# Placing the output matmuls of a two-layer convolution trunk between its projection steps, with the normalisations on VectorE alone

## The chip, the cores and the metric

The kernel runs on the eight cores of one Trainium2 chip. Every core takes one prompt sequence of 2048 tokens and 64 new decode tokens, 2112 tokens in all, and works alone: nothing is exchanged between cores. The time of an execution is that of the slowest core, in microseconds (us), and the figure quoted for a kernel is the median of its runs.

## The reference

```python
def hybrid_layer(x, ...):
    h = rmsnorm(x, norm_g)
    p = einsum('btd,de->bte', h, w_in)            # 1024 -> 7168
    a_val, a_gate, z_a, gb, gc, hb, z_b = split(p, 7 ways)
    u = a_val * sigmoid(a_gate)
    ca = causal_dwconv(u, buf_a, conv_a_w)        # width 31
    ca = head_layernorm(ca + conv_a_b, ...)       # over 128 channels of a head
    y_a = silu(ca) * silu(z_a)
    v = gc * hb
    cb = causal_dwconv(v, buf_b, conv_b_w)        # width 3
    y_b = gb * cb * silu(z_b)
    y = einsum('bte,ed->btd', concat([y_a, y_b]), w_out)   # 2048 -> 1024
    return x + y
# two such layers, then a final rmsnorm; the last rows of u and v are also returned
```

## The kernel before

Channels lie on the partitions, in eight groups of 128, and tokens in the free dimension, in five blocks (four of 424 tokens, the last of 416: 352 prompt and 64 decode tokens). `x_sb` keeps x in float32 and `h_sb` the normalised x in bfloat16, both for all tokens. `y_sb` holds only four groups of 128 gated channels, so the output projection of a layer is done in four rounds of four groups each.

A layer has a part A (eight heads) and a part B (eight channel groups). In part A each head j runs over the five blocks: `a_step` projects the gate, the value and z (8 matmuls each, lines 325 and 333), forms u on VectorE (line 540), and copies u into shifted replicas `rep` with four DMAs of the SP queue (line 557). The convolution of width 31 is done on TensorE (line 450), two blocks at a time, on every second step and two to three steps late; mean, variance, normalisation, silu and the product that writes `y_sb` (`st_mean`, `st_var`, `st_tt`, `st_silu`, `st_y`) follow one stage at a time in later steps. The decode tokens' convolution (`a_samp`, lines 427 to 436) runs on GpSimd (POOL) after a head's last block and writes through `acc_f`, the buffer in which part B also accumulates. In part B each group runs `b_step` over the five blocks: 32 matmuls for z, Bg, C and hb, a three-tap convolution on VectorE into `acc`, and the product into `y_sb`.

After heads 0 to 3, heads 4 to 7, groups 0 to 3 and groups 4 to 7 stands one output stage each, `out_round`: for each block 8 groups of 4 matmuls (one per output channel group m), each followed by an addition into `x_sb` on VectorE (line 401). Within the output stages of part A, `drain_hook` finishes the convolution pipeline at fixed places.

The normalisation has two halves. `rms_stats` squares x on ScalarE (ACT, line 344), sums over the channels with 8 matmuls (line 351), and forms the factor `rr_t` with Ln and Exp (lines 356 and 358). `rms_apply` multiplies: groups 3, 5 and 7 by a product on POOL (line 381) and a scaled copy on ACT (line 384), the others in one instruction on VectorE (line 387); the final one of the kernel also does group 1 in that way for all but the last block, and writes into staging buffers from which one DMA per group (line 391) stores y.

Weights come in tiles of 128x1024 into `NW` slots of `wsl`, with DMAs of the POOL queue (line 310), in the order of the list `wseq`; `w_get_batch(k)` takes the next k slots and starts loads up to `NW` tiles ahead of the batch's start. The order of instructions on every engine is the order in which the Python code calls `P.op`; waits are derived from reads and writes of the named resources. A load or product that waits on POOL holds back whatever stands behind it there, and the same on each engine.

## Time and profile before

| | |
|---|---|
| median of 3 runs | 1334.97 us (1334.41 to 1339.0) |
| the profiled execution | 1334.29 us, span of its slowest core 1332.7 us |
| spans of the eight cores | 1325.8 to 1332.7 us |
| TensorE (PE) busy | 1229.4 us (92%) |
| VectorE (DVE) busy | 753.2 us (57%) |
| ScalarE (ACT) busy | 553.2 us (42%) |
| GpSimd (POOL) busy | 309.9 us (23%) |
| mean granted TensorE clock of the cores | 0.976 to 0.982 |

The span is the time from the first to the last instruction of the slowest core. A busy share is that of all the span, and engines overlap. In the timelines below a line is a run of like instructions: its start, the time it took, engine, line of the kernel, operation, output and inputs, the number of instructions, and in brackets how long the engine had been idle before it and what ended that.

### The profile page before, as it was taken

The page shows a single profiled execution, that of the slowest core. Times are in us where ns is not written, and L with a number is a line of the kernel's source. Part 1 is how long each engine was busy: PE and PEld are TensorE (multiplying, and loading weights), DVE is VectorE, ACT ScalarE, POOL GpSimd, SP SyncE. Part 2 cuts the span into 40 slices and gives each one's busy share as a digit, 9 for nine tenths or more (in the row PEclk, how much of TensorE's full clock was granted, in tenths as well). Part 3 has the DMA queues.
Part 4 walks back from the last instruction along what each step waited for, and adds up shares of the span by engine and source line. Part 5 has one row for each costly group of instructions (what it writes and reads, how often), then busy time and mean ns, then how long its engine had stood idle before and what let it go on. Part 6 is the DMA issues. An engine that isn't in the chain of part 4 may idle for free.

```text
span 1332.7 us, 25104 instructions; the slowest of 8 cores (1325.8 to 1332.7 us)
## 1 busy us (share of the span) xinstructions
PE 1229.4 (92%) x8618; PEld 652.7 (49%) x8618; DVE 753.2 (57%) x1350; ACT 553.2 (42%) x811; POOL 309.9 (23%) x397
## 2 busy tenths in 40 slices
PE   3699999999999999999969999999999999999973
PEld 0245455545455555555524454554545555555530
DVE  2444465343766667666854437443475667666684
ACT  3766652667511110111466766176741111111164
POOL 2353331333401000001144333033341000001033
PEclk9799999999999999999989999999999999999996
DMA  9354443454232321112393543354413321122027
GB/s 249 88 107 93 101 100 72 102 114 101 58 44 42 54 33 33 32 33 43 30 184 74 115 98 65 82 114 97 104 37 44 64 33 32 33 33 44 13 106 164
DMA packets 89579, 102.10 MB, mean 77 GB/s; under 512 B 17328, under 2 KB 70704, under 8 KB 89392
## 3 DMA queue, kind: packets, MB, share of 16 engines
q0 software_dynamic: 20736, 37.76, 18.5%
q1 hardware_dynamic: 67904, 58.67, 17.4%
q10 hardware_dynamic: 816, 4.08, 1.6%
q8 instruction: 72, 1.18, 0.4%
q14 instruction: 51, 0.42, 0.1%
HBM read 92.41 MB, written 13.37 MB: 79 GB/s over the span
## 4 chain that ended last, share of the span: by engine, by line
PE 81%; DMA 5%; ACT 4%; issue 3%; POOL 3%; DVE 2%; SPq 1%; DVEq 0%; ACTq 0%; POOLq 0%
PE ps L325 70%; PE ps L450 8%; DMA rep<-ubuf 3%; PE ps L351 2%; POOL tt_t L381 2%; ACT sq L344 1%; DMA x_sb<-xT 1%; PE ps L463 1%; SPq L557 1%; DVE x_sb L401 1%; PE ps L333 1%; ACT L356 0%; DMA y_fm<-sz_t 0%; POOL acc L433 0%; POOL sz_t L381 0%
## 5 line engine op out<-in xcount | busy, mean ns | idle before, releaser
L325 PE MATMUL ps<-h_sb,wsl 128*128 128x424 bf16 (+1 forms) x4400 | 812.6, 342 | 3.8 <-ACT th_t L529 2.8
L325 PEld LDWEIGHTS ps<-h_sb,wsl 128*128 128x128 bf16 x4400 | 427.1, 98 | 365.5 <-issue 19.9
L325 PE MATMUL ps<-y_sb,wsl 128*128 128x424 bf16 (+1 forms) x1280 | 236.1, 343 | 10.1 <-DVE x_sb L401 5.3
L401 DVE TENSOR_TENSOR x_sb<-x_sb,ps 128x424 f32<-128x424 f32 (+1 forms) x320 | 180.6, 591 | 51.8 <-PE ps L325 33.2
L325 PEld LDWEIGHTS ps<-y_sb,wsl 128*128 128x128 bf16 x1280 | 124.7, 98 | 117.2 <-issue 17.4
L540 DVE SCALAR_TENSOR_TENSOR ubuf<-th_t,ps 128x424 bf16<-128x424 f32 (+1 forms) x80 | 46.6, 583 | 196.3 <-PE ps L325 96.0
L310 POOL DMA_DIRECT2D wsl<-w_in_r x112 | 60.7, 550 | 401.6 <-PE ps L325 386.6
L638 ACT ACTIVATE sz_t<-ps 128x424 f32<-128x424 f32 (+1 forms) x80 | 41.8, 522 | 263.2 <-PE ps L325 263.2
L450 PE MATMUL ps<-rep,wc 128*32 128x424 bf16 (+1 forms) x2560 | 120.4, 340 | 9.6 <-DMA rep<-ubuf 9.5
L427 POOL TENSOR_TENSOR acc<-usam,hista 128x992 f32<-128x992 bf16 x32 | 59.3, 1855 | 280.6 <-DVE oa_t L547 202.2
L669 DVE SCALAR_TENSOR_TENSOR acc<-ubuf,cw_b_sb,acc 128x424 f32<-128x424 bf16 (+1 forms) x192 | 112.1, 584 | 20.8 <-DVE acc L666 1.1
L651 DVE TENSOR_TENSOR ubuf<-ps,th_t 128x424 bf16<-128x424 f32 (+1 forms) x80 | 47.0, 587 | 133.8 <-PE ps L325 133.8
L647 ACT ACTIVATE th_t<-ps 128x424 f32<-128x424 f32 (+1 forms) x80 | 41.8, 522 | 191.7 <-PE ps L325 174.7
L433 POOL TENSOR_TENSOR acc<-acc 128x480 f32<-128x480 f32 (+3 forms) x128 | 92.5, 722 | 18.9 <-POOL acc L433 0.9
L450 PEld LDWEIGHTS ps<-rep,wc 128*32 128x32 bf16 x2560 | 65.5, 97 | 62.9 <-issue 27.8
L529 ACT ACTIVATE th_t<-ps 128x424 f32<-128x424 f32 (+1 forms) x80 | 41.8, 522 | 105.5 <-PE ps L325 95.3
L351 PE MATMUL ps<-sq,ones_s 128*128 128x424 bf16 (+1 forms) x120 | 39.1, 446 | 45.4 <-ACT sq L344 45.4
L493 DVE SCALAR_TENSOR_TENSOR tt_t<-ps,cbias,rstd_t 128x424 f32<-128x424 f32 (+1 forms) x80 | 48.8, 652 | 46.0 <-ACT rstd_t L486 45.8
L455 DVE CAST cb<-ps 128x424 bf16<-128x424 f32 (+1 forms) x80 | 45.5, 578 | 44.2 <-PE ps L450 44.1
L470 ACT ACTIVATE d<-ps,cbias 128x424 bf16<-128x424 f32 (+1 forms) x80 | 48.3, 609 | 51.5 <-PE ps L463 45.4
L387 DVE SCALAR_TENSOR_TENSOR h_sb<-x_sb,vecs_sb,rr_t 128x424 bf16<-128x424 f32 (+1 forms) x50 | 47.5, 1009 | 31.6 <-ACT rr_t L358 31.6
L381 POOL TENSOR_TENSOR tt_t<-x_sb,rr_t 128x424 f32<-128x424 f32 (+1 forms) x33 | 43.3, 1333 | 93.0 <-ACT rr_t L358 76.6
(62 smaller groups left out, 805.0 us busy)
## 6 DMA issues: line engine op xcount, KB each, us to landing
rep<-ubuf SPq DMA_DIRECT2D x256, 113.0 KB, 2.6
wsl<-w_in_r POOLq DMA_DIRECT2D x112, 256.0 KB, 5.8
wsl<-w_out_r POOLq DMA_DIRECT2D x32, 256.0 KB, 5.3
x_sb<-xT SPq DMA_DIRECT2D x16, 424.0 KB, 13.8
rep<-ubuf SPq DMA_DIRECT2D x64, 95.0 KB, 2.3
hista<-hist_a SPq DMA_DIRECT2D x16, 255.5 KB, 3.4
oa_copy<-sa_orig ACTq DMA_DIRECT2D x2, 1664.0 KB, 19.5
y_fm<-sz_t SPq DMA_DIRECT2D x15, 212.0 KB, 2.3
```

Source lines behind the costliest of these rows:

```text
L310: P.op("pool", (lambda e, i=i, s=s: e.dma_start(out=wsl[:, s, :], in_=wseq[i])), writes=[w_r[s]], chan=ch_w[s], name=f"wload{i}")
L325: ins = e.matmul(bank(bk, n), lhsT=l_, rhs=r_, start=(i == 0), stop=(i == len(pairs) - 1))
L351: ins = e.matmul(bank(bk, n), lhsT=ones_s[:], rhs=sq[:, s, i, 0:n], start=(kp == 0 and i == 0), stop=(kp == 3 and i == 1))
L381: P.op("pool", (lambda e, k=k, tmp=tmp: e.tensor_tensor(out=tmp, in0=x_sb[:, k, c0:c0 + n], in1=rr_t[:, rs, 0:n], op=ALU.mult)), reads=[x_ ...
L387: P.op("dve", (lambda e, k=k, dst=dst, gk=gk: e.scalar_tensor_tensor(out=dst, in0=x_sb[:, k, c0:c0 + n], scalar=gk, in1=rr_t[:, rs, 0:n], ...
L401: P.op("dve", (lambda e, bk=bk, m=m, c0=c0, n=n: e.tensor_tensor(out=x_sb[:, m, c0:c0 + n], in0=x_sb[:, m, c0:c0 + n], in1=bank(bk, n), op ...
L427: P.op("pool", (lambda e: e.tensor_tensor(out=prod[:, :, :], in0=win(e), in1=hista[:, UHN:UHN + WA].unsqueeze(2).broadcast_to([128, WA, 32 ...
L433: P.op("pool", (lambda e, n=n, h=h: e.tensor_tensor(out=prod[:, 0:n - h, :], in0=prod[:, 0:n - h, :], in1=prod[:, h:n, :], op=ALU.add)), r ...
L450: ins = e.matmul(psum[32 * q:32 * q + 32, bd, 0:npr], lhsT=w, rhs=rep[:, rp, q, 4 * m:4 * m + npr], start=(m == 0), stop=False, tile_posit ...
L470: P.op("act", (lambda e: e.activation(out=d2[:, i2, 0:n], in_=bank(bd, n), func=AF.Square, bias=cbc)), reads=[bank_r[bd], cbias_r], writes ...
L493: P.op("dve", (lambda e: e.scalar_tensor_tensor(out=tt_t[:, it, 0:n], in0=bank(bd, n), scalar=cbc, in1=rstd_t[:, t, 0:n], op0=ALU.add, op1 ...
L669: P.op("dve", (lambda e, a0=a0, a1=a1, vsl=vsl, wcol=wcol, k=k: e.scalar_tensor_tensor(out=acc[:, iac, a0:a1], in0=vsl(k), scalar=wcol, in ...
```

## The change

- `out_round` and `drain_hook` go. `out_block` does one block of the output matmuls, and is called after a projection step: for heads 0 to 3 after each `a_step` of head 4; for heads 4 to 7 after each `b_step` of group 0; for groups 0 to 3 and 4 to 7 one block behind the `b_step`s of groups 3 and 7, with the last block after them. The list of weights is reordered to match, and `NW` is 10, not 9.
- The stages of the convolution pipeline are gathered in `pipe`, which runs on through all eight heads and the first four steps of group 0 in part B. Steps that share TensorE's output banks with it use banks 0 to 3 only, and so do the output matmuls placed there.
- All normalisations are on VectorE. The final one is written over `x_sb`, and stored with one DMA per two groups.
- The normalisation of layer 1 (and the final one) is done for blocks 0 to 3 within group 7's steps of the part before.

```diff
-NW = 9
+NW = 10
...
+        for j in range(8):
+            wseq.extend(w_in_r[l, c] for c in (8 + j, j, 16 + j))
+            if j == 4:
+                w_out_of(l, 0)
+        for j in range(8):
+            wseq.extend(w_in_r[l, c] for c in (48 + j, 24 + j, 32 + j, 40 + j))
+            if j in (0, 3, 7):
+                w_out_of(l, {0: 4, 3: 8, 7: 12}[j])
...
-                P.op("pool", (lambda e, k=k, tmp=tmp: e.tensor_tensor(
-                    out=tmp, in0=x_sb[:, k, c0:c0 + n], in1=rr_t[:, rs, 0:n], op=ALU.mult)),
-                    reads=[x_r[k][b], rr_r[rs]], writes=[tres])
-                P.op("act", (lambda e, tmp=tmp, dst=dst, gk=gk: e.activation(out=dst, in_=tmp, func=AF.Copy, scale=gk)),
-                     reads=[tres, vecs_r], writes=[dres])
...
+    def final_apply(b, rs, ks=range(KC)):
+        c0, n = BLOCKS[b]
+        for k in ks:
+            P.op("dve", (lambda e, k=k: e.scalar_tensor_tensor(
+                out=x_sb[:, k, c0:c0 + n], in0=x_sb[:, k, c0:c0 + n], scalar=vecs[:, 64 + k:65 + k],
+                in1=rr_t[:, rs, 0:n], op0=ALU.mult, op1=ALU.mult)),
+                reads=[x_r[k][b], rr_r[rs], vecs_r], writes=[x_r[k][b]])
+            if k % 2:
+                P.op("sp", (lambda e, k=k: e.dma_start(out=y_fm[:, k - 1:k + 1, c0:c0 + n], in_=x_sb[:, k - 1:k + 1, c0:c0 + n])),
+                     reads=[x_r[k - 1][b], x_r[k][b]], chan=ch_out[k // 2])
+
+    def out_block(b, slots, next_bank, hook=None):
+        c0, n = BLOCKS[b]
+        for m in range(KC):
+            bk = next_bank()
+            pairs = [(wsl[:, slots[kk], m * 128:(m + 1) * 128], y_sb[:, kk, c0:c0 + n]) for kk in range(4)]
+            mm_group(bk, n, pairs, reads=[w_r[s] for s in slots] + [y_r[kk][b] for kk in range(4)])
+            P.op("dve", (lambda e, bk=bk, m=m: e.tensor_tensor(
+                out=x_sb[:, m, c0:c0 + n], in0=x_sb[:, m, c0:c0 + n], in1=bank(bk, n), op=ALU.add)),
+                reads=[bank_r[bk], x_r[m][b]], writes=[x_r[m][b]])
+            if hook is not None:
+                hook(m)
...
+            slots, _ = w_batch(7 if j == 4 else 3)
...
+                    w_prefetch((6, 9, NW)[b - 2])
+                if j == 4:
+                    ob = Rot([1, 2, 3, 0] if st["g"] % 2 == 0 else [0, 1, 2, 3])
+                    out_block(b, slots[3:7], ob.next)
...
+            outs = j in (0, 3, 7)
+            slots, release = w_batch(8 if outs else 4)
...
+            def out_norm(b):
+                def hook(m):
+                    if j == 7 and b >= 1:
+                        if b == NB - 1 and m == 2:
+                            rs_of[b - 1] = rms_stats(b - 1, pool_all.next())
+                        if m >= 4:
+                            norm(b - 1, rs_of[b - 1], [2 * m - 8, 2 * m - 7])
+                out_block(b, slots[4:8], pool_all.next, hook)
+
+            for b in range(NB):
+                if j == 0:
+                    g = 8 * NB + b
+                    write_y = b_step(l, j, b, slots[0:4], g)
+                    if b == NB - 1:
+                        release(4)
+                    ob = Rot([2, 3, 0, 1] if g % 2 == 0 else [0, 1, 2, 3])
+                    out_block(b, slots[4:8], ob.next)
+                    write_y()
+                else:
+                    b_step(l, j, b, slots[0:4])()
+                    if outs and b == NB - 1:
+                        release(4)
+                    if j == 7 and b >= 2:
+                        rs_of[b - 2] = rms_stats(b - 2, pool_all.next())
+                    if outs and b >= 1:
+                        out_norm(b - 1)
+            if outs and j:
+                out_norm(NB - 1)
```

Where the instructions now stand, at three places (each row is an instruction, or xN like ones; the brackets name semaphores it waits for, `c_w5` being the load into weight slot 5 and `s_pe` TensorE). Line numbers of the changed kernel are its own: its lines 413 to 422 are `a_samp`, 373 the final normalisation, 387 the addition into x.

POOL, from the start of the kernel, before:

```order
L310 DMA wsl<-w_in_r 128x1024 x3
L381 TENSOR_TENSOR tt_t<-x_sb,rr_t 128x424 x12
L310 DMA wsl<-w_in_r 128x1024 x3
L381 TENSOR_TENSOR tt_t<-x_sb,rr_t 128x416 x3
L310 DMA wsl<-w_in_r 128x1024 x3
L427 TENSOR_TENSOR acc<-usam,hista 128x992
```

and in the changed kernel:

```order
L310 DMA wsl<-w_in_r 128x1024 x9
L413 TENSOR_TENSOR acc<-usam,hista 128x992
L419 TENSOR_TENSOR acc<-acc 128x480
L419 TENSOR_TENSOR acc<-acc 128x256
L419 TENSOR_TENSOR acc<-acc 128x128
```

The products of the normalisation that stood between the first loads are gone, so nine loads stand in a row at the start where three did.

POOL at the end of part A of layer 0 (the last decode convolution and the loads behind it), before:

```order
L436 TENSOR_TENSOR cbs<-acc 128x32 [waits s_pool]
L310 DMA wsl<-w_in_r 128x1024 [waits c_w7,s_pe]
L310 DMA wsl<-w_in_r 128x1024 [waits s_pe,c_w8]
L310 DMA wsl<-w_in_r 128x1024 [waits c_w0,s_pe]
L507 TENSOR_TENSOR y_sb<-tt_t,sz_t 128x424 [waits s_act]
```

and in the changed kernel, followed by TensorE at the first step of part B there:

```order
L419 TENSOR_TENSOR acc<-acc 128x64 [waits s_pool]
L422 TENSOR_TENSOR cbs<-acc 128x32 [waits s_pool]
L310 DMA wsl<-w_out_r 128x1024 [waits c_w5,s_pe]
L310 DMA wsl<-w_in_r 128x1024 [waits s_pe,c_w6]
L310 DMA wsl<-w_in_r 128x1024 [waits c_w7,s_pe]
```

```order
L325 MATMUL ps<-h_sb,wsl 128x424 [waits s_act,c_w8]
L325 MATMUL ps<-h_sb,wsl 128x424 x7
L325 MATMUL ps<-d,ones_v 128x424 [waits s_act,s_dve]
L325 MATMUL ps<-d,ones_v 128x424 [waits s_act]
L325 MATMUL ps<-h_sb,wsl 128x424 [waits c_w9]
L325 MATMUL ps<-h_sb,wsl 128x424 x7
L325 MATMUL ps<-h_sb,wsl 128x424 [waits c_w0,s_act]
L325 MATMUL ps<-h_sb,wsl 128x424 x7
L325 MATMUL ps<-h_sb,wsl 128x424 [waits c_w1,s_dve]
L325 MATMUL ps<-h_sb,wsl 128x424 x7
L325 MATMUL ps<-y_sb,wsl 128x424 [waits c_w2,c_w4,c_w3,c_w5,s_act]
```

The load into slot 5, an output weight, stands behind the whole decode convolution on POOL, and the first output matmul of part B waits for it after one step of 34 matmuls; before, the three loads there were for tiles used after a whole output stage.

VectorE at the end of the kernel (the last output block of layer 1 and what follows), before:

```order
L401 TENSOR_TENSOR x_sb<-x_sb,ps 128x416 x8
L387 SCALAR_TENSOR_TENSOR sz_t<-x_sb,vecs_sb,rr_t 128x424 x3
L387 SCALAR_TENSOR_TENSOR tt_t<-x_sb,vecs_sb,rr_t 128x424
L387 SCALAR_TENSOR_TENSOR rstd_t<-x_sb,vecs_sb,rr_t 128x416
L387 SCALAR_TENSOR_TENSOR th_t<-x_sb,vecs_sb,rr_t 128x416
L387 SCALAR_TENSOR_TENSOR sz_t<-x_sb,vecs_sb,rr_t 128x416 x3
```

and in the changed kernel:

```order
L387 TENSOR_TENSOR x_sb<-x_sb,ps 128x416 x5
L373 SCALAR_TENSOR_TENSOR x_sb<-x_sb,vecs_sb,rr_t 128x424 x2
L387 TENSOR_TENSOR x_sb<-x_sb,ps 128x416
L373 SCALAR_TENSOR_TENSOR x_sb<-x_sb,vecs_sb,rr_t 128x424 x2
L387 TENSOR_TENSOR x_sb<-x_sb,ps 128x416
L373 SCALAR_TENSOR_TENSOR x_sb<-x_sb,vecs_sb,rr_t 128x424 x2
L387 TENSOR_TENSOR x_sb<-x_sb,ps 128x416
L373 SCALAR_TENSOR_TENSOR x_sb<-x_sb,vecs_sb,rr_t 128x424 x2
L373 SCALAR_TENSOR_TENSOR x_sb<-x_sb,vecs_sb,rr_t 128x416 x8
```

The last block's additions are now mixed with the eight normalisations of the block before, and eight more follow for the last block where VectorE did five.

## Rows read from the trace of the kernel before

**Rows 1.** Waits of TensorE, whole span: total us, times, longest
```profile
PE ps L351 <- ACT sq L344: 45.4, 23, 7.0
PE ps L450 <- DMA rep<-ubuf: 9.5, 5, 3.1
...
PE ps L325 <- DVE x_sb L401: 6.3, 6, 1.2
PE ps L325 <- POOL y_sb L507: 4.8, 4, 1.3
```

**Rows 2.** Busy time in a 20 us stretch of part B
```profile
540.00:560.00 20.00, 20.00 (x115) 10.96 (x112) 12.70 (x27) 3.80 (x8) 2.11 (x4) 1.00 0.33 54
```

**Rows 3.** DMA issues of the first 30 us: KB each, us to landing
```profile
x_sb<-xT SPq DMA_DIRECT2D x16, 424.0 KB, 13.8
...
wsl<-w_in_r POOLq DMA_DIRECT2D x3, 256.0 KB, 13.3
```

**Rows 4.** Timeline of the first head of layer 0
```profile
43.62 3.03 PE L325 MATMUL ps<-h_sb,wsl 128*128 128x424 bf16 x16
...
44.82 5.47 DVE L387 SCALAR_TENSOR_TENSOR h_sb<-x_sb,vecs_sb,rr_t 128x424 bf16<-128x424 f32 x5 [7.05 <-ACT rr_t L358]
...
49.91 0.50 ACT L569 ACTIVATE sz_t<-ps 128x424 f32<-128x424 f32 x1
...
59.15 1.59 PE L325 MATMUL ps<-h_sb,wsl 128*128 128x424 bf16 x8 [0.88 <-ACT th_t L529]
...
62.35 0.51 ACT L569 ACTIVATE sz_t<-ps 128x424 f32<-128x424 f32 x1
...
66.92 4.42 PE L450 MATMUL ps<-rep,wc 128*32 128x424 bf16 x64
...
71.98 2.89 DVE L387 SCALAR_TENSOR_TENSOR h_sb<-x_sb,vecs_sb,rr_t 128x416 bf16<-128x416 f32 x5
...
79.82 4.66 PE L325 MATMUL ps<-h_sb,wsl 128*128 128x416 bf16 x16
```

**Rows 5.** Timeline of TensorE, first output stage of layer 0 and around it
```profile
84.41 3.05 PE L450 MATMUL ps<-rep,wc 128*32 128x424 bf16 x64
...
183.43 4.46 PE L325 MATMUL ps<-y_sb,wsl 128*128 128x424 bf16 x24
...
218.23 13.06 PE L325 MATMUL ps<-h_sb,wsl 128*128 128x424 bf16 x72
```

**Rows 6.** Timeline of POOL at the same place
```profile
182.69 1.85 POOL L427 TENSOR_TENSOR acc<-usam,hista 128x992 f32<-128x992 bf16 x1 [18.44 <-DVE oa_t L547]
...
194.60 1.66 POOL L310 DMA_DIRECT2D wsl<-w_in_r x3 [0.31 <-issue]
```

**Rows 7.** DMA issued between 193.5 and 195 us, to landing
```profile
wsl<-w_in_r POOLq DMA_DIRECT2D x1, 256.0 KB, 3.9
```

**Rows 8.** Timeline of TensorE from layer 0 into layer 1
```profile
665.80 1.60 PE L333 MATMUL ps<-h_sb,wsl 128*128 128x424 bf16 x8
...
674.43 2.98 PE L333 MATMUL ps<-h_sb,wsl 128*128 128x424 bf16 x8 [3.29 <-DVE ubuf L540]
...
712.79 3.05 PE L450 MATMUL ps<-rep,wc 128*32 128x424 bf16 x64
```

**Rows 9.** Timeline of the last 75 us
```profile
1260.29 9.48 PE L325 MATMUL ps<-y_sb,wsl 128*128 128x424 bf16 x52
...
1264.79 6.66 DVE L401 TENSOR_TENSOR x_sb<-x_sb,ps 128x424 f32<-128x424 f32 x13
...
1291.17 3.29 ACT L344 ACTIVATE sq<-x_sb 128x848 bf16<-128x848 f32 x4
...
1316.94 0.69 SPq L677 DMA_DIRECT2D ob_new<-ob_t  x1
...
1318.07 0.55 ACT L358 ACTIVATE rr_t<-rr_t 128x416 f32<-128x416 f32 x1
```

**Rows 10.** DMA issues from 1309 us on
```profile
ob_new<-ob_t SPq DMA_DIRECT2D x1, 256.0 KB, 11.0
```

More of the change, by code:

```diff
@@ L268, in build_nc @@
     ch_rep = [chan(f"rep{i}") for i in range(NR)]
-    ch_out = [chan(f"out{i}") for i in range(NTH + NSZ + 4)]
+    ch_out = [chan(f"out{i}") for i in range(4)]
     ch_oa = chan("oa")
@@ L515, in a_step @@
         sg, sv, szw = st["slots"]
-        odd = g % 2
         last = b == NB - 1
         npr = NPL if last else n
-        bg, bv, bz = (1, 2, 3) if odd else (0, 1, 0)
-        pair = []
-        if odd and len(q_conv) >= 2:
-            pair = [q_conv.pop(0), q_conv.pop(0)]
-            for s in pair:
-                st_conv(s)
-            while q_y:
-                st_y(q_y.pop(0))
+        bg, bv, bz = (1, 2, 3) if g % 2 else (0, 1, 0)
+        pipe(0, g)
         proj(sg, b, bg, by_k)
@@ L559, in a_step @@
         rep_r[rp].w = P.ops["sp"][-1]
[L560 to L566 removed]
+        pipe(2, g)
         proj(szw, b, bz)
@@ L632, in b_step @@
         s_zb, s_gb, s_gc, s_hb = slots
-        bzb = pool_all.next()
+        if g is None:
+            bzb, bgb, bgc, bhb = [pool_all.next() for _ in range(4)]
+        else:
+            bzb, bgb, bgc, bhb = (2, 3, 2, 3) if g % 2 else (0, 1, 0, 1)
+            pipe(0, g)
         proj(s_zb, b, bzb)
@@ L639, in b_step @@
              reads=[bank_r[bzb]], writes=[sz_r[isz]])
-        bgb = pool_all.next()
+        if g is not None:
+            pipe(1, g)
         proj(s_gb, b, bgb)
@@ L643, in b_step @@
              reads=[bank_r[bgb], sz_r[isz]], writes=[sz_r[isz]])
-        bgc = pool_all.next()
+        if g is not None:
+            pipe(2, g)
         proj(s_gc, b, bgc)
@@ L686, in build_nc, with w_batch @@
     rs_of = {}
+    def w_batch(k):
+        start = wstate["next"]
+        return w_get_batch(k), (lambda dead: w_prefetch(start + dead + NW))
     for l in range(DEPTH):
```

217 lines of the change are left out of this document (69 added, 148 removed).

## The prediction

> **What bounds the kernel now.** I read the busy shares first, then the waits of TensorE, then its timeline at each place where the program changes its shape. TensorE is busy for 92% of the span, and inside a stage of part B nothing holds it: 114 to 115 matmuls in 20 us at the full clock, 0.175 us each, while VectorE is busy for 12.7 of the 20 us and ACT for 3.8 [rows 2]. The work of TensorE is the same in both kernels, so the change can only win or lose at the seams. The reader is to see four kinds of seam. Statistics of x that wait for the squares of ACT cost 45.4 us in 23 waits; the output stages of part A cost 6.3 us of waits for VectorE's additions and 4.8 for POOL's products; five convolutions wait for their replicas, 9.5 us [rows 1]. The rest is idle time and low clock at the start, from layer 0 to layer 1, and at the end [rows 4, 8, 9].
>
> **The change, part by part.** All against the profiled execution's 1334.3 us, which is 0.7 us below the median of the runs shown.
>
> *Start.* With the scaled copies off ACT, the silu of z no longer waits for them. In one step the projection of z ended at 46.65 and its silu began at 49.91, 3.3 us later; in the next it ended at 60.74 and the silu began at 62.35, 1.6 later [rows 4]. The squares of the next statistics stand behind that silu on ACT, and TensorE behind the squares, so both come off the path, and about 1 us in the step before them. From the first convolution at 66.92 to the next at 84.41 are 17.5 us [rows 4, 5], for 52 matmuls at 0.175 and one pair of convolutions of 3.0, 12.1 us in all; of the 5.4 lost, part is waiting for ACT's copies and part matmuls at half rate (16 in 4.66 us at 79.82, against 3.03 at 43.62 [rows 4]). I take 4. VectorE's eight multiplications cost no more than its five did: five took 5.47 us with POOL at work beside them, and 2.89 us, 0.58 each, without [rows 4], so eight are 4.6. Block 1's squares can start up to 4 us earlier, if x is there; against that, POOL now issues nine weight loads at once instead of three, and the first three, sharing the DMA engines with x, took 13.3 us to land while the x transfers took 13.8 [rows 3]. I take 2 for this. Start: minus 12. Ends: minus 16 if the loads disturb nothing, 0 if x is late by all of them (six loads at about 1.9 us, from three that land within 6 us of one another's issue at 194.60).
>
> *Output stages of part A.* One stage spans 183.43 to 218.23, 34.8 us [rows 5], for 165 matmuls and a pair of convolutions, about 32. The waits behind the difference are the 6.3 and 4.8 us of [rows 1]. After head 4's steps the same matmuls find four banks that are read at once and products that were written a step earlier, with VectorE needed for some 7 of 12 us of a step. Minus 11; ends minus 11 and minus 5.
>
> *Replicas.* Four of the five waits fall on the third step after a weight load that starts when POOL has finished the decode convolution; heads 2 and 6 keep that phase. One goes, minus 2 (0 to minus 4).
>
> *Layer 0 to layer 1.* From 665.80 to 712.79 are 47.0 us [rows 8] for 140 matmuls and 3.0 of convolutions, 27.5: 19.5 us lost to four normalisations between the projection steps. In the changed kernel one is left there. It costs 2.8: silu 0.5, first square 0.8, then three squares at 0.82 (four take 3.29 [rows 9]) against two matmuls at 0.35. Three more now stand right behind a `b_step`, where ACT starts squaring while TensorE still does the 1.4 us of hb: 1.5 us of idle time each, 4.5. The fourth meets a VectorE that is behind: four additions at 0.51 (13 take 6.66 [rows 9]) and eight multiplications at 0.58 against 2.8 us of matmuls leave the last addition of block 3 about 3.4 us late, 2.7 us idle; and the first u of layer 1 queues behind the rest, 1.2. Loss 11.2, gain 8 (3 to 12). VectorE is not the bound before that: 3.5 + 4.1 + 4.6 = 12.2 us a step, TensorE 12.6 + 1.5.
>
> *End.* All projections end at 1260.3 [rows 9]. From there, with four output blocks and three statistics, 152 matmuls at 0.177 and 4.5 idle: block 3 is out at E = 1291.7. Then VectorE sets the time. Its last addition for block 3 comes at E + 3.4, the factor for block 3 at E + 6.1, and the mixed row of additions and multiplications runs on to the last addition of block 4 at E + 12.1; squares, sums, Ln and Exp give the last factor at E + 14.9 = 1306.6, against 1318.6 [rows 9]. Eight multiplications end at E + 19.5. The last transfers: before, 14.1 us passed from factor to end, and the `ob_new` store issued at 1316.94 took 11.0 us to land [rows 9, 10]; now it is issued at E + 14.5 and would land at E + 25.5, with the last pairs of groups about then. End at 1317.2, minus 15.5. Ends: 14.1 us after the factor as before, minus 12; last store landed 2.6 us after its product, minus 19.
>
> *What it adds: the first output matmul of part B waits for its weight.* The group needs four tiles; the fourth is loaded by POOL only after the decode convolution of head 7. At the same place of the loop before, the last projection of the head ended at 183.4 [rows 5], POOL had begun the convolution at 182.69 and issued its next load at 194.60, 11.2 us after that end [rows 6], and the first tile landed 3.9 us later [rows 7]: 15.1 to 15.5. TensorE has 34 matmuls until then, 6.0 us. So 9.4 us of idle time in each layer, behind which everything in part B stands, since nothing else is queued on TensorE. Before, those loads had a whole output stage to hide them, 34.8 us [rows 5]; that cover is gone. `acc`, which the decode convolution holds as well, is free earlier and costs nothing more. After an idle time of 3.3 us the next 8 matmuls took 2.98 us, at the lower of the clock's two levels, in place of 1.4 [rows 8]: 2 us more here. Then each of the five steps has four banks for its output matmuls and VectorE does the v product and three taps first, 2.4 + 0.6 us before the first bank is free against 2.8 of matmuls: 0.3 a step, 1.5 a layer. Plus 13 a layer, 26; ends plus 20 and plus 32.
>
> Sum: −12 − 11 − 2 − 8 − 15.5 + 26 = −22.5, so **1312**.
>
> **A rule that speaks against it.** What the rows show is that three loads and the transfers of x were in flight together for 13 us [rows 3]; my 2 us for the start supposes that x loses little to six more. The Trainium skill (DMA: Bandwidth & Descriptors, section on queues, rings and completion order) says that each DMA engine goes round robin, packet by packet, between the queues that have work. By that rule the six loads are taken in while x is still arriving, x comes later by up to their whole time, and the sum would be 1324 in place of 1312. No run here shows nine loads at once.
>
> **The rivals.**
> - *x late by all six loads.* For: DMA engines are saturated there and POOL has nothing between the loads. Against: the ACT chain, not the arrival of x, sets the steps after block 1. The start gains nothing: 1324. Chance 0.13.
> - *No stall at part B.* If the tile came in time, the 20 us and their clock would not be paid: about 1289. For it only that a load can be faster than the one seen; against it 11.2 us of POOL's work in front of it. 0.06.
> - *VectorE becomes the bound in group 7's steps.* If a multiplication costs 1.09 us (5.47 for five [rows 4]) also there, a step needs 16.3 us of VectorE against 14.1 of TensorE, in three steps of two layers, and the end loses 8: 13 + 8 = 21, 1333. Against: POOL, which ran beside those five, only issues loads there. 0.11, of which a third stops short at about 1326.
> - *Slower: TensorE falls to 1.2 GHz in the mixed steps of part B.* The idle time comes at their head, and short bank waits follow in each step. The ten steps are some 120 us at the full clock; with half of that time's work at the lower level they cost 60 more: 1372. It turns the result from 29 us on, which is a quarter of the work there. For: matmuls at half rate after 3.3 us idle [rows 8]. Against: the next 16 there ran at full rate. 0.08.
>
> **How the numbers follow.** The forecast itself has 0.62, and its own bounds taken together give 1301 to 1323. The range for 8 in 10 reaches a little past them to the case of late x: 1299 to 1326. A measurement of this kernel can tell about 0.5% from no change, 6.7 us, so faster means below 1328.3: 0.62 + 0.13 + 0.06 + 0.04 = 0.85. Same: 0.07. Slower: 0.08.
>
> **What would show it.** In the profile of the changed kernel: two waits of TensorE, 8 to 11 us each, at the first output matmul of part B, ended by a weight load; no wait for POOL's products; the first convolution near 56 us and not 66.9; one normalisation's wait of some 3 us after layer 0; the last factor near 1307 less what the rest moved (so 14 us or less before the end). The prediction is wrong if those two waits are under 5 us, if the first convolution stays at 66, if the clock stays low in the mixed steps, or if VectorE's multiplications cost over 0.8 us.

## The result, and the profile after

The changed kernel takes **1367.9 us** (median of 4 runs) against 1335.2 for the one before on the same chip: ratio 1.0235, interval 1.0210 to 1.0261. It is slower by 33 us where 22.5 less was forecast, and lies outside the range. In some executions of any of these kernels the cores of one die or both show a lower granted clock and the time is longer (here the fourth, 1387.0); ratios and intervals leave these out, the medians do not. The profiled execution took 1368.1 us, with a span of 1366.5 on its slowest core.

TensorE's waits in the changed kernel (us in total, times, longest), beside [rows 1]:

```profile
PE ps L351 <- ACT sq L344: 40.3, 46, 3.8
PE ps L436 <- DMA rep<-ubuf: 31.0, 7, 8.7
PE ps L325 <- DMA wsl<-w_out_r: 18.8, 2, 9.5
...
PE ps L325 <- DVE x_sb L387: 8.2, 10, 1.6
PE ps L325 <- ACT sz_t L564: 3.2, 6, 0.7
```

The two waits for an output weight are the predicted ones (9.4 each), and the one for POOL's products is gone. What the sum did not have is the second line: the convolutions' replicas cost 31.0 us where they cost 9.5. Four places on TensorE's timeline of the changed kernel show the largest of these waits and one of the two for the tile, with what follows them:

```profile
260.35 3.02 PE L436 MATMUL ps<-rep,wc 128*32 128x424 bf16 x32 [8.13 <-DMA rep<-ubuf]
...
361.33 8.27 PE L325 MATMUL ps<-y_sb,wsl 128*128 128x424 bf16 x32 [9.30 <-DMA wsl<-w_out_r]
...
720.47 5.05 PE L436 MATMUL ps<-rep,wc 128*32 128x424 bf16 x64 [8.66 <-DMA rep<-ubuf]
...
910.18 3.02 PE L436 MATMUL ps<-rep,wc 128*32 128x424 bf16 x32 [5.40 <-DMA rep<-ubuf]
```

The number in brackets is the idle time before the row. The 32 matmuls after 9.30 us of it took 8.27, and 32 at the full rate take 5.8 (52 in 9.48, [rows 9]): the idle time costs 2.4 us more behind itself. The convolutions pay likewise: 64 matmuls took 5.05 us where 64 take 3.05 [rows 5]. In front of the first row, at head 5 of layer 0, the DMA traffic of the changed kernel from 243 to 262 us reads so (KB each, us to landing):

```profile
q0 software_dynamic: 1008, 1.84, 62.9%
q1 hardware_dynamic: 1126, 0.91, 16.9%
...
wsl<-w_in_r POOLq DMA_DIRECT2D x7, 256.0 KB, 10.1
rep<-ubuf SPq DMA_DIRECT2D x8, 113.0 KB, 9.9
```

POOL issues seven loads in a row there, at 243.89: head 4 now uses seven tiles (three projections and four of output), and head 5 refills their slots at once. The replica copies in flight with them need 9.9 us. The wait before 910.18 is that of head 5 in layer 1. In front of 720.47 it is another transfer (688 to 722 us of the changed kernel):

```profile
q10 hardware_dynamic: 96, 3.41, 54.3%
q0 software_dynamic: 576, 1.05, 17.9%
q1 hardware_dynamic: 1808, 1.56, 14.6%
...
oa_copy<-sa_orig ACTq DMA_DIRECT2D x2, 1664.0 KB, 19.1
rep<-ubuf SPq DMA_DIRECT2D x12, 113.0 KB, 16.1
wsl<-w_in_r POOLq DMA_DIRECT2D x4, 256.0 KB, 23.3
```

The queues' rows are packets, MB and share of the DMA engines: `oa_copy` (q10) moves 3.41 MB in 96 packets, 35 KB each, beside weight loads (q0) of 1.8 KB a packet and replicas (q1) of 0.9, which take 16 us to land. It was issued at the same point of the program before, within the last block of output matmuls, but then the first convolution of layer 1 was further away. The copy and that convolution in the kernel before, and the copy in the changed kernel:

```profile
664.58 1.32 ACTq L742 DMA_DIRECT2D oa_copy<-sa_orig  x2
...
697.55 3.14 PE L450 MATMUL ps<-rep,wc 128*32 128x424 bf16 x64
```

```profile
690.21 1.33 ACTq L728 DMA_DIRECT2D oa_copy<-sa_orig  x2
```

Before, 33.0 us lay between them; in the changed kernel TensorE has nothing else to do from 711.8 on, 21.6 us after the issue, because three of the four normalisations no longer stand between these steps. It was the normalisations that covered the copy, not an output stage.

The start: the first two convolutions of the changed kernel stand at 67.93 and 80.87, where [rows 4, 5] have 66.92 and 84.41, so 3.5 us are won of the 12.

```profile
67.93 3.66 PE L436 MATMUL ps<-rep,wc 128*32 128x424 bf16 x64
...
80.87 3.05 PE L436 MATMUL ps<-rep,wc 128*32 128x424 bf16 x64
```

That is what the prediction named as a sign of being wrong: the first convolution is not near 56. In its first 45 us x shares the DMA engines with nine weight loads. From 15 to 30 us the engines (last two columns: their busy share and GB/s) read so in the changed kernel, and, below it, in the experiment start_loads, where only three loads are issued before x has landed:

```profile
15.00:30.00 15.00, 2.59 (x6) 0.41 (x6) 5.75 (x9) 4.72 (x6) 0.00 (x0) 1.00 1.05 220
```

```profile
15.00:30.00 15.00, 9.29 (x28) 2.92 (x28) 7.69 (x14) 8.73 (x12) 0.00 (x0) 1.00 1.00 306
```

The engines are busy throughout in both, but with the nine loads they move 220 GB/s in all and not 306: x loses the bytes of the six extra loads and part of the rate besides.

The end: the last block's factor and what follows it, in the changed kernel, beside [rows 9, 10]:

```profile
1351.02 0.79 SPq L639 DMA_DIRECT2D ob_new<-ob_t  x1
1351.56 0.55 ACT L358 ACTIVATE rr_t<-rr_t 128x416 f32<-128x416 f32 x1
1352.21 4.59 DVE L373 SCALAR_TENSOR_TENSOR x_sb<-x_sb,vecs_sb,rr_t 128x416 f32<-128x416 f32 x8 [2.20 <-ACT rr_t L358]
1353.49 4.16 SPq L378 DMA_DIRECT2D y_fm<-x_sb  x4
```

The multiplications cost 0.57 us each as forecast. From the factor (1352.1) to the end are 14.4 us, as before (14.1), not the 11 of the sum.

Where the 33 us are, by landmarks that both kernels have: the second convolutions of the two layers (80.87 above and 734.80, for 84.41 and 712.79 in [rows 5, 8]) and the first projection of group 4 of part B, before and then after:

```profile
518.00 114.40 PE L325 MATMUL ps<-h_sb,wsl 128*128 128x424 bf16 x640
...
1146.05 114.40 PE L325 MATMUL ps<-h_sb,wsl 128*128 128x424 bf16 x640
```

```profile
537.75 97.31 PE L325 MATMUL ps<-h_sb,wsl 128*128 128x424 bf16 x544
...
734.80 3.05 PE L436 MATMUL ps<-rep,wc 128*32 128x424 bf16 x64
...
1190.08 97.31 PE L325 MATMUL ps<-h_sb,wsl 128*128 128x424 bf16 x544
```

Both stretches to group 4 get half of the sum's terms for the output stages, the replicas and part B.

| stretch | before | changed | difference | forecast |
|---|---|---|---|---|
| start to second convolution, layer 0 | 84.4 | 80.9 | -3.5 | -12 |
| to group 4 of part B, layer 0 | 433.6 | 456.9 | +23.3 | +6.5 |
| to second convolution, layer 1 | 194.8 | 197.1 | +2.3 | -8 |
| to group 4 of part B, layer 1 | 433.3 | 455.3 | +22.0 | +6.5 |
| to the end | 186.7 | 176.4 | -10.2 | -15.5 |

### The profile page after: what moved, and what is told of

Same layout as the page of the kernel before. It is cut to its first block, busy times and chain, and to the rows that moved or that the text cites. A ratio compares the mean times of both kernels' runs of the same rounds, so it can differ in the third digit from the quotient of the medians.

```text
span 1366.5 us, 24760 instructions; the slowest of 8 cores (1355.9 to 1366.5 us)
## 1 busy us (share of the span) xinstructions
PE 1234.1 (90%) x8618; PEld 652.9 (48%) x8618; DVE 747.3 (55%) x1407; ACT 531.2 (39%) x768; POOL 236.5 (17%) x340
## 4 chain that ended last, share of the span: by engine, by line
PE 76%; DMA 8%; DVE 5%; ACT 4%; issue 3%; POOL 1%; SPq 1%; DVEq 0%; ACTq 0%; POOLq 0%
PE ps L325 66%; PE ps L436 8%; DMA rep<-ubuf 5%; DMA x_sb<-xT 2%; ACT sq L344 2%; DVE x_sb L387 2%; SPq L558 1%; PE ps L333 1%; DVE x_sb L373 1%; PE ps L449 1%; POOL acc L419 1%; DVE h_sb L365 1%; PE ps L351 1%; DMA wsl<-w_out_r 1%; POOL acc L413 1%
## 5 line engine op out<-in xcount | busy, mean ns | idle before, releaser
L325 PE MATMUL ps<-y_sb,wsl 128*128 128x424 bf16 (+1 forms) x1280 | 241.4, 346 | 29.7 <-DMA wsl<-w_out_r 18.8
L387 DVE TENSOR_TENSOR x_sb<-x_sb,ps 128x424 f32<-128x424 f32 (+1 forms) x320 | 176.2, 589 | 32.5 <-PE ps L325 21.6
L597 ACT ACTIVATE sz_t<-ps 128x424 f32<-128x424 f32 (+1 forms) x80 | 41.8, 522 | 323.3 <-PE ps L325 311.4
L436 PE MATMUL ps<-rep,wc 128*32 128x424 bf16 (+1 forms) x2560 | 126.1, 350 | 31.0 <-DMA rep<-ubuf 31.0
L351 PE MATMUL ps<-sq,ones_s 128*128 128x424 bf16 (+1 forms) x120 | 35.6, 392 | 40.6 <-ACT sq L344 40.3
L602 DVE TENSOR_TENSOR sz_t<-ps,sz_t 128x424 f32<-128x424 f32 (+1 forms) x80 | 47.4, 593 | 31.4 <-PE ps L325 29.7
```

Source lines behind the costliest of these rows:

```text
L325: ins = e.matmul(bank(bk, n), lhsT=l_, rhs=r_, start=(i == 0), stop=(i == len(pairs) - 1))
L351: ins = e.matmul(bank(bk, n), lhsT=ones_s[:], rhs=sq[:, s, i, 0:n], start=(kp == 0 and i == 0), stop=(kp == 3 and i == 1))
L387: P.op("dve", (lambda e, bk=bk, m=m: e.tensor_tensor(out=x_sb[:, m, c0:c0 + n], in0=x_sb[:, m, c0:c0 + n], in1=bank(bk, n), op=ALU.add)), ...
L436: ins = e.matmul(psum[32 * q:32 * q + 32, bd, 0:npr], lhsT=w, rhs=rep[:, rp, q, 4 * m:4 * m + npr], start=(m == 0), stop=False, tile_posit ...
L602: P.op("dve", (lambda e: e.tensor_tensor(out=sz_t[:, isz, 0:n], in0=bank(bgb, n), in1=sz_t[:, isz, 0:n], op=ALU.mult)), reads=[bank_r[bgb] ...
```

## The experiments

Theory: the placement is harmless, and what costs is that four sets of transfers and one tile come at the wrong moment. Rival: the placement between steps itself, by its banks, its statistics and TensorE's clock. Each run was timed beside the kernel before on the same chip. The medians of before were 1334.8 us for the first four runs and 1335.0, 1333.2 and 1339.7 for the later ones, so runs of different sets are compared by ratio; a ratio less by 0.001 is 1.3 us.

| run | us | ratio to before | interval |
|---|---|---|---|
| changed kernel | 1367.9 | 1.0235 | 1.0210 to 1.0261 |
| tile_early | 1360.4 | 1.0194 | 1.0180 to 1.0208 |
| loads_paced | 1350.4 | 1.0114 | 1.0099 to 1.0129 |
| copy_late | 1359.2 | 1.0188 | 1.0175 to 1.0202 |
| start_loads | 1362.7 | 1.0202 | 1.0185 to 1.0219 |
| tile_early_acc | 1350.2 | 1.0116 | 1.0101 to 1.0132 |
| ob_early | 1364.6 | 1.0232 | 1.0217 to 1.0247 |
| all_five | 1307.9 | 0.9796 | 0.9783 to 0.9810 |
| before_dve_norm | 1308.1 | 0.9818 | 0.9798 to 0.9839 |
| all_six | 1306.1 | 0.9796 | 0.9776 to 0.9815 |
| norm_paced | 1288.2 | 0.9651 | 0.9629 to 0.9673 |
| norm_plain | 1318.8 | 0.9891 | 0.9873 to 0.9910 |
| six_banks | 1296.6 | 0.9700 | 0.9668 to 0.9731 |
| stats_mid | 1300.6 | 0.9727 | 0.9700 to 0.9754 |
| all_nine | 1292.1 | 0.9656 | 0.9623 to 0.9690 |
| norm_over_x | 1295.2 | 0.9683 | 0.9652 to 0.9714 |

### One cause at a time

**tile_early.**
```diff
         if last:
+            if j == 7:
+                w_prefetch(wstate["next"] - 3 + NW + 1)
             a_samp(0)
```


> Changed kernel, with the eighth tile of part B's first group loaded before the decode convolution of head 7 in POOL's program instead of after it. Late tile theory: the two waits for the w_out tile (9.3 and 9.5 us) go. In their place stays what the decode convolution still holds, the accumulators of VectorE's taps, behind which the additions of the output blocks are queued: POOL is done 11.2 us after the last projection, TensorE has 32 matmuls (5.6 us) and four banks (2.8 us) until then, so a wait of 3 to 5 us for VectorE. Gain 5 a layer and 1 to 2 of clock: 1356 (1353 to 1360) against 1367.9. Rival, that the accumulators alone would hold TensorE as long: 1366 to 1368, with waits of 8 us or more for VectorE at the same place.

Measured 1360.4, by ratio 5.5 us under the changed kernel. The waits for the tile are gone; `acc` takes their place, as one row of VectorE's waits (345 to 385 us) and one of TensorE's timeline in this run show:

```profile
DVE acc L630 <- POOL cbs L422: 3.0, 1, 3.0
```

```profile
359.67 4.71 PE L325 MATMUL ps<-y_sb,wsl 128*128 128x424 bf16 x16 [3.51 <-DVE x_sb L387]
```

**tile_early_acc.**
```diff
-        iac = rot_acc.next()
+        if g is None:
+            iac, av, ar = rot_acc.next(), acc, acc_r
+        else:
+            iac, av, ar = rot_rr.next(), rr_t, rr_r
```
(and `av`, `ar` for `acc`, `acc_r` in the taps and the product)

> The kernel of run tile_early (1360.4 us), and in part B's first group the products with the taps are kept in the two buffers of the normalisation factor, which nothing uses there, instead of in the buffers that the decode convolution of head 7 holds. If those buffers are what VectorE still waits for (its wait for POOL was 3.0 us at the first tap, TensorE's for VectorE's additions behind it 3.5 and 4.9 us): these waits go, and the matmuls at half rate behind them: minus 9 (7 to 12), 1351. Rival, that the four banks and VectorE's own work at this place make the same wait, whoever holds the buffers: minus 0 to 3, 1358 to 1360.

Measured 1350.2, another 10 us. The prediction's sentence that `acc` "costs nothing more" held only while the tile was late as well: tile and buffers are the same 9.4 us, held by the same decode convolution.

**loads_paced.**
```diff
+                if paced and 1 <= b <= 3:
+                    w_prefetch(goal - (todo * (3 - b)) // 3, [rep_r[st["rep"]]])
```
(`goal` is what the head's start would have loaded, `todo` how many that is; the list is what the load waits for)

> Changed kernel, with the weight loads of part A's heads 1 to 7 not issued all at the head's start but spread over its second to fourth block, each waiting until the replicas of that block have landed. Collision theory (the loads that head 5 issues seven in a row take the DMA engines from the replica copies): the waits for replicas at heads 5 and 6 (8.1, 2.5, 1.7 us in layer 0; 5.4, 2.8 in layer 1) fall under 1 us each, and the matmuls at half rate behind them go: minus 20 (16 to 25), 1348. The wait of 8.7 at the start of layer 1 and the two for the w_out tile stay (or grow by up to 1 us). Rival, that the copies wait for their queue on SP or for the u of VectorE, whatever POOL loads: no change of those waits, 1366 to 1369.

Measured 1350.4, with the layer 1 wait left alone, as expected, in TensorE's waits of this run:

```profile
PE ps L325 <- DMA wsl<-w_out_r: 20.0, 2, 11.3
PE ps L436 <- DMA rep<-ubuf: 12.0, 3, 7.8
```

So some 16 us (17.5 by the medians) were paid to loads that nothing needed at once. The edit spreads the loads of all these heads and not only head 5's; of the changed kernel's waits, the 8.1 and 5.4 us behind the seven loads are the largest that went. The rival falls: same copies, same SP queue, other loads.

**copy_late.**
```diff
-        if l == 0:
-            for l2 in range(DEPTH):
-                P.op("act", ... oa_copy[l2] ...)
+                if l == 1 and b == 4 and j in (1, 2):
+                    P.op("act", ... oa_copy[j - 1] ...)
```


> Changed kernel, with the two oa_copy transfers (3.4 MB, from memory to memory) issued in part B of layer 1 instead of just before the first step of layer 1. If oa_copy is what the first replicas of layer 1 collide with: the wait of 8.7 us at 720.47 falls to 0 to 2 and its matmuls at half rate go: minus 9 (7 to 11), 1359. If the four weight loads issued at 693.60 do as much by themselves: the wait stays at 4 us or more, 1363 to 1367. Should oa_copy disturb the place where it now stands, a wait for a weight tile shows there; none is expected, since part B has no replicas.

Measured 1359.2, by ratio 6.3 us less. On the slowest core the first convolutions of layer 1 then start without a wait:

```profile
712.44 4.15 PE L436 MATMUL ps<-rep,wc 128*32 128x424 bf16 x64
```

The four weight loads beside it, still there, do no harm that can be seen. The rule by which the prediction argued (the Trainium skill, DMA: Bandwidth & Descriptors, section on queues, rings and completion order: each engine takes the queues in turn, packet by packet) fits this. With turns by packet, 35 KB against 0.9 leaves little for the replicas. No run here changes the packet size alone.

**start_loads.**
```diff
-                    w_prefetch((6, 9, NW)[b - 2])
+                    w_prefetch((6, 9, NW)[b - 2], [x_r[7][NB - 1]])
```


> Changed kernel, with the seven weight loads that POOL issues during the first head of layer 0 made to wait until the last piece of x has landed. If the loads are what makes x late: the last x piece lands 6 to 10 us earlier, block 1's squares start earlier, and the first two convolutions (67.93 and 80.87) move forward by 6 to 9: 1360 (1357 to 1363). Rival, that x is limited by its own 20 issues on SP, which take 39.7 us: no change in either landmark, 1367 to 1369.

The first convolutions moved by 10.2 us, to where the prediction had wanted the first (56):

```profile
57.71 3.67 PE L436 MATMUL ps<-rep,wc 128*32 128x424 bf16 x64
...
70.66 3.05 PE L436 MATMUL ps<-rep,wc 128*32 128x424 bf16 x64
```

The time fell by 5.2 only, and by ratio by 4.4, with intervals that just overlap; the waits for replicas are still there and a core's come out differently (8.7 to 13.4 us in layer 0 in this run, on two cores). The pair norm_plain and before_dve_norm below shows the same edit at 9.7 us by ratio.

**ob_early.** `b_finish(l)` stands right behind the last `b_step`.

> Changed kernel, with the two stores of ob issued as soon as the last step of part B has made their data, before the stores of y for block 3, and not between those of block 3 and block 4. If the end is set by what all stores of the last 15 us move together: the 0.26 MB of ob_new in 1024 pieces leave the last stretch, the four stores of block 4 land in 6 to 8 us instead of 8.9, minus 2 (1 to 4): 1366. Rival, that the four stores of block 4 take 8.9 us by themselves: no change, 1367 to 1369.

Median 1364.6, but the intervals of the ratio overlap: no gain in time is shown by this run. Its profile does show the mechanism. The last four stores, from issue to landing, in the changed kernel and in this one:

```profile
y_fm<-x_sb SPq DMA_DIRECT2D x4, 416.0 KB, 8.9
```

```profile
y_fm<-x_sb SPq DMA_DIRECT2D x4, 416.0 KB, 2.5
```

The end comes 7.8 us after the factor, not 14.4, so the rival falls. In all_five it comes 8.1 us after it.

### All of it, and the other half of the change by itself

> Changed kernel with all of it together: paced loads (now also in head 0 of layer 1), oa_copy in part B of layer 1, the seven first loads after x, the eighth tile before head 7's decode convolution with separate buffers for part B's first taps, and the ob stores early. If the losses are separate places that add up: 1367.9 minus 7.5, 17.5, 8.7 and 5.2 as measured one by one, minus 9 for the buffers and 2 for the ob stores: 1318 (1312 to 1324), faster than the kernel before. The waits for replicas are then under 1 us each, those for the w_out tile gone, and what is left of TensorE's waits is the statistics' 30 to 40 us. Rival, that the placement of output matmuls between steps costs something of its own (banks, clock), which the waits hid: 1330 to 1345, with the clock under 0.98.

Measured 1307.9. The edits are those above together, with the pacing in every head of part A but the first (`l + j > 0`). This is below the expected range: taken as measured (with 10.2 for the buffers and 3.3 for the ob stores) the losses promised 1316, and by ratio only 1323. Together they gain 8 to 15 us more than one by one, and which of them does isn't shown; the pacing of head 0 of layer 1, new here, is one candidate. The next run shows that as much can be won without the placement.

**before_dve_norm.**
```diff
-            rms_apply(0, 0, rs_of[0], split=(3, 5, 7))
+            rms_apply(0, 0, rs_of[0])
```
(and so in the four other calls; the first loads wait for `x_r[7][NB - 1]`)

> Kernel before, its output stages as they were, with the normalisations all on VectorE (final ones too, through their staging buffers as before) and the six loads that would then be issued at once made to wait for the last piece of x. This is the part of the change that the prediction gave 12 us at the start. If that mechanism is right and only the loads spoiled it in the changed kernel: the first convolution moves from 66.92 to 56 to 58 and the time falls by 8 to 12: 1325 (1322 to 1328). If the start is bound by x and nothing is won: 1334. At the end eight multiplications on VectorE in place of a split between two engines may cost up to 2.

Measured 1308.1: minus 27 (24 by ratio), and not 8 to 12, with the old output stages, the old loads but for the first six, and the old `oa_copy`. The places, in its timeline (TensorE and, last, the end of its statistics):

```profile
69.80 3.05 PE L450 MATMUL ps<-rep,wc 128*32 128x424 bf16 x64
...
167.84 4.46 PE L325 MATMUL ps<-y_sb,wsl 128*128 128x424 bf16 x24
...
696.30 3.05 PE L450 MATMUL ps<-rep,wc 128*32 128x424 bf16 x64
...
1243.15 7.15 PE L325 MATMUL ps<-y_sb,wsl 128*128 128x424 bf16 x39
...
1283.83 0.85 PE L351 MATMUL ps<-sq,ones_s 128*128 128x416 bf16 x2 [0.48 <-ACT sq L344]
```

Against 84.41 and 183.43 [rows 5] the start gives 15; from there to 712.79 [rows 8] two more; and from the first output matmul of the last stage (1260.29 [rows 9]) to the last sum this kernel takes 41.5 us, where the one before took 57 (its factor follows at 1318.07). Of this 10.8 reach the end of the kernel. The rest is lost behind the last sum, where 20.1 us pass to the end instead of 15.3, with the `ob` stores still in front of the last ones (in norm_paced below, with these issued early, 10.4). Without scaled copies ACT squares while TensorE works, and TensorE's waits for squares go from 45.4 to this:

```profile
PE ps L351 <- ACT sq L344: 23.6, 29, 2.8
PE ps L450 <- DMA rep<-ubuf: 13.4, 5, 5.2
```

**norm_plain** is the same without the guard on the loads.

> The kernel of run before_dve_norm (1308.1 us) without the wait for x in front of the six first loads, so that nine are issued at once as in the changed kernel. If they make x late also here: the first convolution goes from 56.7 to 62 to 67, and the time rises by 4 to 7: 1313 (1311 to 1316), still faster than the kernel before. Rival, no difference: 1307 to 1309.

Measured 1318.8: the loads cost 9.7 us here by ratio (10.7 by the medians). This is the normalisation half of the change as it was written, and it is 1.1% faster than the kernel before; the other half is then what loses 46 us (ratio 1.0235 less 0.9891). The guard on the loads was not tried on the kernel before by itself, so what it would give with the old normalisations stays open.

**all_six** moves one more load.
```diff
-        if l == 0:
-            P.op("act", ... histb ...)
+                if l == 0 and j == 6 and b == 3:
+                    P.op("act", ... histb ...)
```
Its reason is a row of all_five, of VectorE's waits from 320 to 345 us:

```profile
DVE ubuf L581 <- DMA histb<-hist_b: 9.3, 1, 9.3
```

> The kernel of run all_five (1307.9 us), and the load of part B's history issued in head 6 of part A instead of at the start of part B. In all_five VectorE waits 9.3 us for that load at part B's first step, TensorE 6.0 us behind it (333.77), and 8 matmuls at half rate follow. If nothing else holds that place: these go, minus 7 to 8, 1300 (1297 to 1303). Rival, that the next thing (the accumulators, the banks) makes a wait of its own of 4 us or more there: 1304 to 1308.

Measured 1306.1, ratio unchanged. The wait for the history is gone, others stand in its place on the slowest core (TensorE's timeline in layer 0 and 1):

```profile
335.26 4.55 PE L325 MATMUL ps<-y_sb,wsl 128*128 128x424 bf16 x16 [2.18 <-DVE x_sb L387]
...
899.21 0.31 PE L449 MATMUL ps<-cb,ones_n 128*128 128x352 bf16 x1 [4.53 <-POOL cbs L422]
```

The second is made by my own pacing: the load of the fourth block waits for its replicas, and the decode convolution is queued behind it on POOL.

**norm_paced** is before_dve_norm, so with the old output stages, and with the diffs of loads_paced, copy_late and ob_early.

> The kernel of run before_dve_norm (1308.1 us; output stages of their own), and with it the paced loads of part A, oa_copy in part B of layer 1 and the ob stores early, that is the same cures as in all_five and all_six but without the placement of output matmuls between steps. Its waits for replicas (13.4 us, 5.2 of it at 681.73) and the half rate behind them go, and some of the last stores' time: 1297 (1294 to 1301). The difference to all_six is what the placement between steps is worth by itself: by the prediction's terms for the output stages of part A and for part B's banks some minus 8, which would leave this kernel behind all_six by as much; if it is worth nothing, the two agree within 3 us.

Measured 1288.2, 3.5% under the kernel before, and 18 under all_six, on the same chip: with its transfers mended, the placement still costs 18 us, where the expectation had it ahead by 8. By the landmarks of both profiles (slowest cores): second convolution 68.62 against 71.73; from there to the same convolution in layer 1 618.0 against 624.3; from there to the last sum 589.7 against 599.7. The first of these is not the placement's: both kernels start alike but for one weight load, and on the cores of these two profiles that convolution comes anywhere from 68.6 to 71.8.

### What the placement costs

**six_banks** and **stats_mid**, each on all_six:
```diff
-                    ob = Rot([2, 3, 0, 1] if g % 2 == 0 else [0, 1, 2, 3])
+                    ob = Rot([[2, 3, 4, 5, 0, 1, 4, 5], [0, 1, 4, 5, 2, 3, 4, 5], [2, 3, 4, 5, 6, 7, 0, 1],
+                              [0, 1, 4, 5, 6, 7, 2, 3], [2, 3, 0, 1, 4, 5, 6, 7]][b])
```
```diff
-                        if b == NB - 1 and m == 2:
+                        if m == 2:
                             rs_of[b - 1] = rms_stats(b - 1, pool_all.next())
...
-                    if j == 7 and b >= 2:
-                        rs_of[b - 2] = rms_stats(b - 2, pool_all.next())
```


> The kernel of run all_six (1306.1 us), with the output matmuls in part B's first group going round six to eight banks instead of four. If the banks are the cost: the ten waits for VectorE's additions there (0.6 to 2.2 us, some 13 in all) fall to 4 or less, minus 9: 1297 (1295 to 1300). Rival, that VectorE is behind by its own work and the wait only moves to the next projection: minus 0 to 3, 1303 to 1306.

> The kernel of run all_six, with the sums of the squares in head 7 of part B placed behind the third output matmul group of the next block instead of right behind the projection step. If TensorE waits there because ACT starts to square only then (four waits of 0.24 to 0.28 us a statistics and matmuls of 2 in 0.8 us instead of 0.35): each statistics gains 1.8, three in each layer, minus 9: 1297 (1295 to 1300). Rival, that the factor comes later and VectorE's multiplications with it, so that the end is pushed out: 1304 to 1308.

By ratio 0.0096 (12.8 us) and 0.0069 (9.2 us) under all_six. TensorE's waits for VectorE's additions in six_banks, 13.0 in all_six:

```profile
PE ps L325 <- DVE x_sb L387: 4.0, 4, 1.8
```

And one statistics of the last stretch, first in all_six, then in stats_mid:

```profile
1259.58 0.52 PE L351 MATMUL ps<-sq,ones_s 128*128 128x424 bf16 x2 [0.28 <-ACT sq L344]
1260.38 0.52 PE L351 MATMUL ps<-sq,ones_s 128*128 128x424 bf16 x2 [0.28 <-ACT sq L344]
```

```profile
1256.87 1.60 PE L351 MATMUL ps<-sq,ones_s 128*128 128x424 bf16 x8
```

In the first TensorE gets two matmuls every 0.8 us, at ACT's pace; in the second all eight run in 1.6.

**all_nine** has both, and `if paced and b <= 2` in place of `1 <= b <= 3`.

> The kernel of run all_six with both (six_banks and stats_mid) and the paced loads one block earlier, so that the decode convolution no longer stands behind a load that waits for the fourth block's replicas. If these three are the 18 us by which the placement is behind: minus 9, 9 and 3 (the 4.5 us wait for POOL at 899.21 goes): 1286 (1282 to 1290), level with norm_paced. If something else costs it: 1295 or more.

Ratio 0.9656, beside 0.9651 for norm_paced: level, within the 4 us or so that these intervals can tell. The three together are the 18 us, though less than their sum (12.8, 9.2 and the expected 3), and the earlier loads were not tried alone. They don't win anything beyond the old stages either.

**norm_over_x** is norm_paced with `final_apply` of the changed kernel, and the same pacing as all_nine.

> The kernel of run norm_paced (1288.2 us; output stages of their own, normalisations on VectorE), with the final normalisation written over x and stored in pairs of channel groups, as in the changed kernel, and the paced loads one block earlier. The end takes as long by the profile of both (10.4 us from the last sum to the end), so the first does nothing: minus 0 to 2; the paced loads: minus 1 to 2 for the waits behind POOL and VectorE: 1286 (1283 to 1289).

Ratio 0.9683, with an interval that overlaps norm_paced's. Written over x or through staging buffers: no gain is shown, and a loss of a few us isn't excluded.

## Why the prediction was wrong

- *Stall at part B's first output matmul, plus 26:* right in place, cause and size (9.3 and 9.5 us for 9.4; the half rate behind it 2.4 for 2). Its side remark on `acc` was wrong (above). Its banks were priced 1.5 a layer and cost 4.1 (8.2 us in ten waits); in all_six the waits for additions are 13.0 us, nearly all there, and six_banks gains 9 to 13.
- *Replicas, minus 2:* **this step failed, and it alone turns the sign.** I looked at the phase of the waits and took the loads as they had been: three or four at a time. The change makes head 4 use seven tiles, so head 5 issues seven loads, and it takes three of the four normalisations away that lay between `oa_copy` and layer 1's first convolution. The waits went from 9.5 to 31.0 us, plus 21.5 where minus 2 stood, and the half rate behind four of them adds some 6 (3.02 us for 1.62 three times, 5.05 for 3.05). The two cures, each by itself, gain 22 us by ratio and 26 by the medians. With plus 28 in this place the sum is plus 7; what is missing to the measured 33 is the start, the output stages with the banks, and the end.
- *Start, minus 12:* the mechanism was right, and larger than priced (15 in before_dve_norm); the six early loads took it back. Of the two prices weighed, 2 us and all of it, the second was near: 10 us at the first convolution. That rival was named, with 0.13, and by it the sum would have been 1324. Its rule from the Trainium skill (DMA: Bandwidth & Descriptors, section on queues, rings and completion order: the queues are taken in turn, packet by packet) agrees with the trace in that x comes later while the loads are taken in; that the whole rate falls too, 220 GB/s for 306, the rule does not say.
- *Output stages of part A, minus 11:* less than half of it, and lost again. If the tile, the banks and the replicas are taken off the two stretches of plus 23.3 and plus 22.0, an estimated minus 5 is left; the banks cost 8.2 where 3 were priced, and all_six, with its tiles in time, takes 6.3 us more over layer 0 than norm_paced. What the stages lose (up to 1.3 us a wait [rows 1]) the placement loses in banks and silus.
- *Layer 0 to 1, minus 8:* the size was right, and it belongs to the normalisations. From the end of part B's first group to the second convolution of layer 1 the changed kernel takes 311.4 us against 309.5, with 8.7 of wait for `oa_copy` and 2 of half rate in it: minus 9 without them. Before_dve_norm has the same gain without the placement, and loses it to the same wait (5.2 us, then 64 matmuls in 5.30 us instead of 3.05): 27.0 us lie there between the issue of the copy and the end of TensorE's other work, where the kernel before had 33.0 and the changed one 21.6.
- *End, minus 15.5:* measured minus 10.2. The factor comes 10.5 us earlier against group 4, for 12 in the sum; the statistics behind each step go at ACT's pace. The end after the factor is as long as before and not 3.5 shorter, because the two `ob` stores go out right before the last four stores and all of them land together 9 to 11 us later. Before_dve_norm gained 10.8 there with the old stage, so the placement itself gives nothing at the end.
- *The rivals:* VectorE as bound did not come, nor did TensorE at 1.2 GHz through the ten mixed steps: in the changed kernel the last column but two, the granted clock, is 0.93 over the stretch with the stall, and full behind it. The forecast of 0.08 for slower named the wrong mechanism; 1367.9 being near its 1372 is chance.

```profile
350.00:425.00 75.00, 61.20 (x374) 32.04 (x375) 44.67 (x86) 13.99 (x21) 9.78 (x17) 0.93 0.19 28
425.00:560.00 135.00, 135.00 (x758) 73.95 (x757) 86.03 (x167) 19.82 (x38) 9.44 (x18) 1.00 0.24 40
```

## What to carry to other kernels

When a change moves work between stages, list every transfer by the gap between its issue and the next wait that shares the DMA engines with it: the output stage that was taken away was the cover of the history load and of a weight tile, the normalisations that went were that of `oa_copy`, and the larger batch of tiles became a burst of seven loads. Loads that are early enough anyway should be issued one by one, behind the small copies that are urgent. And take a change apart before judging it: here one half wins 1.1% as written and 3.5% with its transfers in order, while the other half hides it under 46 us, and no gain of its own is shown when it is mended.

## What the runs showed of the hardware that I had not expected

- Two transfers of 1.7 MB from memory to memory, in 35 KB packets, held up replica copies of 113 KB for 16 us (2.6 us without them, in copy_late), while the four weight loads of 256 KB in 1.8 KB packets cost no wait when they stood there alone. Whether the size of the copies or that of their packets does it, no run separates.
- Nine weight loads beside 8.7 MB of x delay the first convolution by 10 to 12 us (57.71 to 67.93; 56.74 to 68.79 in the pair before_dve_norm and norm_plain). The 1.57 MB of the six extra ones would take 6.8 us at the 232 GB/s that flowed in the first 45 us; the rest fits the lower rate of both together, 220 GB/s for 306 from 15 to 30 us.
- ACT, 42% busy, was the hidden bound of the kernel before at its start and its end: taking three scaled copies out of eight from it, and the work of POOL before them, gave 24 to 27 us with one more edit to the loads, where its waits at the start had shown 12.
- Stores in small pieces hold up what is behind them: the two `ob` stores move 0.27 MB, with over 2000 packets under 512 B in flight at the end of the changed kernel, and four stores of 416 KB behind them land after 8.9 us; with the two issued some 20 us earlier (ob_early), the four land after 2.5 us.
